# A three-part network on one core: norms split into two stages, both layers written out, and the shift out of PSUM shared by ScalarE and VectorE

## The chip, the cores and the metric

The kernel runs on one core of one Trainium2 chip. The metric is the device time of one execution in microseconds. TensorE is PE here, its weight loads are PEld, VectorE is DVE, ScalarE is ACT, GpSimd is POOL, and SyncE, which issues most transfers, is SP.

## What is computed

An input x of 256 tokens by 1024 features goes through two layers of one kind, then a middle part with two other mixers, then eight experts and a last norm. Everything is float32. Of the reference, cut to what matters here:

```python
for l in range(DEPTH):                                   # 2 layers
    mod = c_act @ w_ada[l] + b_ada[l]                    # 6 vectors of 1024
    sh1, sc1, gt1, sh2, sc2, gt2 = jnp.split(mod, 6, axis=-1)
    h = x * (1.0 + sc1) + sh1
    y = _token_mixer(h, w_in[l], b_in[l], ...)           # three kinds of attention
    x = _layernorm(ALPHA * x + gt1 * y, ln_g[l, 0], ln_b[l, 0])
    h = x * (1.0 + sc2) + sh2
    y = _conv_ffn(h, w_up[l], w_conv[l], b_conv[l], w_down[l])
    x = _layernorm(ALPHA * x + gt2 * y, ln_g[l, 1], ln_b[l, 1])
```

The middle part has the same frame without modulation: mixer, norm, FFN, norm, attention, norm, router.

## The kernel before

**Products.** Each float32 weight tile of 1 MB (128 x 2048) is split into a high and a low part: ACT copies it rounded to `W_high` (`high`, L1413), DVE subtracts that from the raw tile and writes `W_low` over it (`low`, L1780), both in two halves. Activations are split in the same way, and a product is three matmuls (L762 to L764). SP loads the tiles into a ring of four slots `W` in the order of the list `W_LOADS` (L631), and in between rows of biases, gains and so on into a ring of four slots `R` (L636); it stops at the first load whose slot is not free. `W_high` has two slots, and ACT waits until PE is done with the tile before the last. PSUM has eight banks, given out in a ring in the order in which PE's jobs stand.

**Modulation.** `w_ada` comes in twelve chunks of 512 columns. DVE multiplies and adds a chunk in eight steps (`ada`, L1825 and L1827); PE sums over the partitions (`ada_column` L877 for shifts and scales, which land as columns in `modc`; `ada_row` for gates). Chunks 0 to 3 are the first thing in a layer and come through the ring `W`. Chunks 4 to 9 stand between the first six chunks of the mixer's input product ("A" and "B"), 10 and 11 between the `down` tiles; these come through two slots of their own, which POOL loads (L732).

**One layer.** PE transposes x (`transposes`, L819), ACT applies scale and shift on the way out of PSUM, four activations a bank (L1434), and rounds the result to `hT_high` (L1438); DVE makes `hT_low` (L1800) bank by bank. A bank holds one token block of 128 (t = 0, 1) and four of the eight feature tiles (q = 0, 1). Then come the A and B chunks, attention with the C and gate chunks in the background, the projections, the `out` product, and DVE's `residual` and `layernorm("ln1")`. After it x is transposed again, and `up` (22 tiles) and `down` (11 tiles, 22 rows of four 512-wide banks) follow, with `hidden_conv` on DVE for each up tile. The layer ends with `residual` and `layernorm("ln2")`. The two layers are one loop on every engine; the middle part is straight code.

**The norm.** `residual` takes the four banks one by one (L1913, L1915, and the statistics L1872). `layernorm` joins the statistics (L1880, L1882), ACT takes the root (L1473), DVE inverts and normalises both token blocks whole (L1886), and multiplies by the gain and adds the bias, half by half (L1894, L1896). Only then does `h_ready` let PE transpose that half.

The `down` loop closes all four banks with its last row:

```python
                        for j, (_, t, n) in enumerate(jobs):
                            last = product(acc[j][:, :], ...
```

## Time and profile before

| | us |
|---|---|
| median of 3 runs (lowest, highest) | 3110.49 (3108.21, 3115.19) |
| the profiled execution | 3112.35 |
| its span on the core | 3110.7 |
| PE busy in the span | 2692.7 (87%) |
| DVE busy | 2210.7 (71%) |
| ACT busy | 1471.9 (47%) |
| mean granted clock of PE | 0.908 |

The profiled execution's time is 1.65 us over its span, which is launch and end. PE's and DVE's busy times are spread unevenly: from about 2090 us on, the experts keep PE at 99 to 100% and the transfers at 320 to 370 GB/s; before that PE has stretches without work between the stages.

### The profile page before, as it was taken

The page shows a single profiled execution, that of the slowest core. Times are in us where ns is not written, and L with a number is a line of the kernel's source. Part 1 is how long each engine was busy: PE and PEld are TensorE (multiplying, and loading weights), DVE is VectorE, ACT ScalarE, POOL GpSimd, SP SyncE. Part 2 cuts the span into 40 slices and gives each one's busy share as a digit, 9 for nine tenths or more (in the row PEclk, how much of TensorE's full clock was granted, in tenths as well). Part 3 has the DMA queues.
Part 4 walks back from the last instruction along what each step waited for, and adds up shares of the span by engine and source line. Part 5 has one row for each costly group of instructions (what it writes and reads, how often), then busy time and mean ns, then how long its engine had stood idle before and what let it go on. Part 6 is the DMA issues. An engine that isn't in the chain of part 4 may idle for free.

```text
span 3110.7 us, 39930 instructions
## 1 busy us (share of the span) xinstructions
PE 2692.7 (87%) x13946; PEld 2286.7 (74%) x13946; DVE 2210.7 (71%) x2764; ACT 1471.9 (47%) x1677; POOL 19.6 (1%) x38
## 2 busy tenths in 40 slices
PE   5888877976888769968888996759999999999997
PEld 4766757965666659958787975658888888888885
DVE  6666656868666657855576545459889898898986
ACT  3243434423244334425333423337777777777774
POOL 0000000000000000000000000000000000000000
PEclk7899988987899889978898987669999999999998
DMA  8633335558533335533204563129898898898985
GB/s 316 253 139 122 137 121 179 185 184 310 215 127 122 132 125 190 198 128 109 82 15 146 178 228 119 55 97 363 343 364 341 340 365 340 337 366 339 370 337 210
DMA packets 104027, 670.75 MB, mean 216 GB/s; under 512 B 11920, under 2 KB 12048, under 8 KB 26432
## 3 DMA queue, kind: packets, MB, share of 16 engines
q1 hardware_dynamic: 98032, 629.95, 54.8%
q0 software_dynamic: 5840, 38.80, 3.3%
q8 instruction: 90, 1.47, 0.2%
q14 instruction: 65, 0.53, 0.0%
HBM read 664.51 MB, written 4.19 MB: 215 GB/s over the span
## 4 chain that ended last, share of the span: by engine, by line
PE 52%; DVE 16%; PEld 16%; issue 8%; ACT 5%; DMA 2%; DVEq 0%; PEldq 0%; SPq 0%; ACTq 0%
PE bank L762 15%; PE bank L763 15%; PE bank L764 15%; PEld bank L764 5%; PEld bank L762 5%; PEld bank L763 5%; DVE W_low L1780 4%; PE bank L1064 3%; DVE work L1827 2%; ACT W_high L1413 1%; DMA W<-in_w_expert 1%; ACT scores L1459 1%; PEld bank L1295 1%; DVE scores L1967 1%; PE bank L819 1%
## 5 line engine op out<-in xcount | busy, mean ns | idle before, releaser
L1780 DVE TENSOR_TENSOR W_low<-W,W_high 128x1024 fp32r<-128x1024 f32 (+2 forms) x448 | 519.9, 1203 | 373.3 <-ACT W_high L1413 366.3
L1413 ACT ACTIVATE W_high<-W 128x1024 fp32r<-128x1024 f32 (+2 forms) x448 | 442.9, 1037 | 669.1 <-PE bank L764 272.0
L763 PE MATMUL bank<-W_low,arena_parts 128*128 128x512 f32 x1224 | 481.9, 394 | 0.0
L762 PE MATMUL bank<-W_high,arena_parts 128*128 128x512 f32 x904 | 365.0, 404 | 26.9 <-DVE work L2282 20.2
L762 PE MATMUL bank<-W_high,hT_high 128*128 128x512 f32 (+4 forms) x784 | 322.6, 412 | 47.0 <-DVE arena L1767 19.0
L764 PE MATMUL bank<-W_high,arena_parts 128*128 128x512 f32 x904 | 357.2, 395 | 0.0
L762 PE MATMUL bank<-hT_high,W_high 128*128 128x256 f32 x1184 | 344.3, 291 | 13.7 <-DVE hT_low L1800 11.8
L763 PE MATMUL bank<-hT_low,W_high 128*128 128x256 f32 x1184 | 340.2, 287 | 0.0
L764 PE MATMUL bank<-hT_high,W_low 128*128 128x256 f32 x1184 | 339.9, 287 | 0.0
L763 PE MATMUL bank<-W_low,hT_high 128*128 128x512 f32 (+4 forms) x784 | 311.5, 397 | 0.0
L764 PE MATMUL bank<-W_high,hT_low 128*128 128x512 f32 (+4 forms) x784 | 310.6, 396 | 0.0
L762 PE MATMUL bank<-arena_parts 128*128 128x512 f32 x672 | 272.5, 406 | 1.9 <-DVE arena_parts L2762 1.9
L763 PEld LDWEIGHTS bank<-W_low,arena_parts 128*128 128x128 f32 x1224 | 233.2, 191 | 48.5 <-issue 1.0
L764 PE MATMUL bank<-arena_parts 128*128 128x512 f32 x672 | 263.8, 392 | 0.0
L762 PEld LDWEIGHTS bank<-hT_high,W_high 128*128 128x128 f32 x1184 | 232.6, 196 | 14.9 <-issue 12.6
L763 PEld LDWEIGHTS bank<-hT_low,W_high 128*128 128x128 f32 x1184 | 233.3, 197 | 0.0
L764 PEld LDWEIGHTS bank<-hT_high,W_low 128*128 128x128 f32 x1184 | 232.5, 196 | 0.0
L763 PE MATMUL bank<-arena_parts 128*128 128x512 f32 x576 | 225.3, 391 | 0.0
L762 PEld LDWEIGHTS bank<-W_high,hT_high 128*128 128x128 f32 x784 | 162.7, 208 | 83.6 <-DVE arena L1767 20.3
L1445 ACT ACTIVATE arena_parts<-W 128x2048 fp32r<-128x2048 f32 x96 | 184.4, 1920 | 81.7 <-DMA W<-in_w_expert 63.0
L762 PEld LDWEIGHTS bank<-W_high,arena_parts 128*128 128x128 f32 x904 | 172.8, 191 | 65.0 <-issue 22.7
L1787 DVE TENSOR_TENSOR W_low<-W,arena_parts 128x2048 fp32r<-128x2048 f32 x96 | 217.9, 2283 | 3.0 <-ACT arena_parts L1445 3.0
(338 smaller groups left out, 4491.1 us busy)
## 6 DMA issues: line engine op xcount, KB each, us to landing
W<-in_w_expert SPq DMA_DIRECT2D x192, 1024.0 KB, 4.8
W<-in_w_layer SPq DMA_DIRECT2D x178, 1024.0 KB, 5.0
arena<-in_w_expert SPq DMA_DIRECT2D x144, 1024.0 KB, 4.8
W<-in_w_middle SPq DMA_DIRECT2D x58, 1024.0 KB, 5.0
arena<-in_w_layer POOLq DMA_DIRECT2D x32, 1024.0 KB, 7.6
R<-in_rows_layer SPq DMA_DIRECT2D x70, 256.0 KB, 5.8
R<-in_rows_middle SPq DMA_DIRECT2D x18, 256.0 KB, 6.1
spread<-arena POOLq DMA_DIRECT2D x1, 3072.0 KB, 11.9
```

Of the source, the lines that this page charges most:

```text
L762: mm(bank, lhs[0], rhs[0], start=start, stop=False)
L763: mm(bank, lhs[0], rhs[1], start=False, stop=False)
L764: return mm(bank, lhs[1], rhs[0], start=False, stop=stop)
L819: last = turn_over(bank[:, i * P:(i + 1) * P], src[:, t, f:f + P], ident)
L1064: last = mm(bank[:, i * P:(i + 1) * P], lhs(i), rhs(i), start=True, stop=True)
L1295: last = turn_over(bank[:, i * P:(i + 1) * P], hid_tok[:, c % 2, i * P:(i + 1) * P], ident)
L1413: do(high_slot(a.at, w)[:, cols], raw(a.at, w)[:, cols], ACT.Copy).then_inc(main_highs.filled[main_highs.slot(a.at, w)], 1)
L1445: do(expert_high(j), expert_raw(j), ACT.Copy).then_inc(stream.raised, 1)
L1459: i = do(scores[:, b, m, 0:K], scores[:, b, m, 0:K], ACT.Exp, bias=nmax[:, b, m:m + 1], accum_out=rsum[:, b, m:m + 1])
L1780: tt(lows(v.at, w)[:, cols], raw(v.at, w)[:, cols], high_slot(v.at, w)[:, cols].bitcast(F32), ALU.subtract).then_inc(*low_ready.event(v.at))
L1787: tt(expert_low(j), expert_raw(j), expert_high(j).bitcast(F32), ALU.subtract).then_inc(stream.lowered, 1)
L1827: i = stt(acc, part, csil[:, f:f + 1], acc, ALU.mult, ALU.add)
```

## The change

- **Both layers are written out** (`layer0`, `layer1`), each with its own lists of loads.
- **The modulation of the next layer moves into this layer's FFN.** Layer 0 computes, after chunks 10 and 11, also chunks 0 to 3 of layer 1 (called `next`), in steps of one DVE instruction placed between up tiles and between down tiles (`ada_steps`), and loads them over POOL's queue. Chunks 10 and 11 move from the down tiles to the up tiles.
- **The norm has two stages.** `norm` only subtracts the mean and divides, in four quarters, each with its own signal to PE. Gain and bias are folded into the modulation (`fold`), or are taken from columns in the middle part (`lnc`), and applied with it on the way out of PSUM. `scale_x`, which multiplies x itself by gain and adds bias, comes later: in the up tiles 0 and 1, or behind the transposes. `residual` joins the statistics of token block 0 before it takes the last bank.
- **Out of PSUM**: ACT scales and shifts token block 1 (`high_shifted`), DVE block 0 (`shifted`); ACT rounds both. This holds for all seven norms with a product behind them, also those of the middle part, where ACT had copied the bank to `hT_high` directly.
- **`down`** keeps its order for nine tiles; the last two tiles are done bank by bank, so that the banks close one after the other.
- **The first two weight tiles behind a norm** are split before the norm, with their high part in a free piece of the arena (`EARLY`, `high_next`, `low_next`).
- **SP** loads rows two tiles later than before, and loads the constants and x at the start behind the first two tiles of chunk 0. The lambda row is handled behind chunk A0. The convolution taps are copied aside. The output goes out in two halves.

The core of the diff:

```diff
+LAYERS = tuple(f"layer{l}" for l in range(DEPTH))
+PASSES = (("start", 1),) + tuple((p, 1) for p in LAYERS) + (
+    ("middle", 1), ("expert", NE - 1), ("last", 1), ("over", None), ("end", 1))
...
+    for j in range(FF1 // P):
+        loads += [("up", j, 0)]
+        if j in (9, 10):
+            loads += [("ada", j + 1, i) for i in range(2)]
+        if j > 10 and j % 2 == 0 and j < 18 + 2 and l + 1 < DEPTH:
+            loads += [("next", NEXT[(j - 12) // 2], i) for i in range(2)]
+    return loads + _halves("down", FF1 // 256, 1)
...
+        EARLY = {("layer0", ("up", 0, 0)): 10256, ("layer0", ("up", 1, 0)): 12304,
+                 ("layer1", ("up", 0, 0)): 10256, ("layer1", ("up", 1, 0)): 12304,
+                 ("layer1", ("A", 0, 0)): 2048, ("layer1", ("A", 0, 1)): 16400,
+                 ("middle", ("ba", 0, 0)): 2048, ("middle", ("qkv", QKV[0], 0)): 16400,
+                 ("middle", ("up", 0, 0)): 6144, ("middle", ("up", 1, 0)): 8192,
+                 ("middle", ("wq", 0, 0)): None}
...
+                    if name == ("ada", 0, 1):
+                        first()
+                    while due and due[0][1] <= 0:
+                        row(due.pop(0)[0])
+                    if name[:2] in R_LOADS[at.part] and name[:2] + (1 - name[2],) not in loads[n:]:
+                        due.append((name[:2], 2))
...
+            def first_inputs():
+                sp.dma_start(consts[:, :], ins["constants"]).then_inc(consts_in, 16)
+                sp.dma_start(x[:, :, :], ins["x"].rearrange("(t p) d -> p t d", p=P)).then_inc(x_in, 16)
...
+                for c in range(tiles // 2 - 2):
+                    for k in (2 * c, 2 * c + 1):
+                        ready(k)
+                        for j in range(4):
+                            last = row(k, j)
...
+                    last.then_inc(*weights.frees(at, ("down", c, 0)))
+                    between(c)
+                for j in range(4):
+                    for k in range(tiles - 4, tiles):
+                        if j == 0:
+                            ready(k)
+                        last = row(k, j)
+                        if j == 3 and k == tiles - 3:
+                            last.then_inc(*weights.frees(at, ("down", tiles // 2 - 2, 0)))
+                    last.then_inc(*psum.fills(at, jobs[j]))
...
+            def high_shifted(name, scale, shift):
+
+                for q in range(2):
+                    f = slice(4 * q, 4 * q + 4)
+                    act.wait_ge(*psum.full(a.at, (name, 1, q)))
+                    bank = banks[psum.slot(a.at, (name, 1, q))]
+                    for i in range(4):
+                        n = 4 * q + i
+                        o = do(hT[:, n, P:S], bank[:, i * P:(i + 1) * P], ACT.Identity,
+                               scale=modc[:, scale + n:scale + n + 1], bias=modc[:, shift + n:shift + n + 1])
+                    o.then_inc(*psum.frees(a.at, (name, 1, q)))
+                    for t in range(NT):
+                        act.wait_ge(*psum.vacated(a.at, (name, t, q)))
+                        cols = slice(t * P, (t + 1) * P)
+                        do(hT_high[:, f, cols], hT[:, f, cols], ACT.Copy).then_inc(*group_high.event(a.at))
...
+            def roots():
+
+                for t in range(NT):
+                    state["var"] += 1
+                    act.wait_ge(*var_ready.nth(a.at, state["var"]))
...
+            def shifted(name, scale, shift):
+
+                for q in range(2):
+                    dve.wait_ge(*psum.full(v.at, (name, 0, q)))
+                    bank = banks[psum.slot(v.at, (name, 0, q))]
+                    for i in range(4):
+                        f = 4 * q + i
+                        o = ts(hT[:, f, 0:P], bank[:, i * P:(i + 1) * P], scale[:, f:f + 1], shift[:, f:f + 1],
+                               ALU.mult, ALU.add)
+                    o.then_inc(*psum.frees(v.at, (name, 0, q)))
+                    for t in range(NT):
+                        state["group"] += 1
+                        dve.wait_ge(*group_high.nth(v.at, state["group"]))
+                        f, cols = slice(4 * q, 4 * q + 4), slice(t * P, (t + 1) * P)
+                        tt(hT_low[:, f, cols], hT[:, f, cols], hT_high[:, f, cols].bitcast(F32), ALU.subtract
+                           ).then_inc(*group_split.event(v.at))
...
+            def ada_steps(l):
+
+                chunks = [("ada", 10), ("ada", 11)] + [("next", c) for c in NEXT if l + 1 < DEPTH]
+                for m, (kind, c) in enumerate(chunks):
+                    acc = ada_acc[:, m % 2, :]
+                    if m > 1:
+                        dve.wait_ge(*psum.full(v.at, chunks[m - 2] if m < 4 else ("next", m - 4)))
+                    for f in range(KD):
...
+            def fold(g, b, sh, sc, to):
+
+                tt(modc[:, to:to + 8], modc[:, g:g + 8], modc[:, sc:sc + 8], ALU.mult).then_inc(dve_done, 1)
+                dve.wait_ge(dve_done, v.count())
+                tt(modc[:, to + 8:to + 16], modc[:, b:b + 8], modc[:, sc:sc + 8], ALU.mult).then_inc(dve_done, 1)
+                dve.wait_ge(dve_done, v.count())
+                tt(modc[:, to + 8:to + 16], modc[:, to + 8:to + 16], modc[:, sh:sh + 8], ALU.add).then_inc(dve_done, 1)
...
+            def norm(signal=None):
+
+                def invert(t):
+                    state["std"] += 1
+                    dve.wait_ge(*std_ready.nth(v.at, state["std"]))
+                    V.reciprocal(inv[:, t:t + 1], inv[:, t:t + 1]).then_inc(dve_done, 1)
                     dve.wait_ge(dve_done, v.count())
...
+                        if n == 0:
+                            invert(t)
+                        half = x[:, t, n * 512:(n + 1) * 512]
+                        i = ts(half, half, meanvar[:, t, 0:1], inv[:, t:t + 1], ALU.subtract, ALU.mult)
+                        if signal is None:
+                            i.then_inc(dve_done, 1)
+                            dve.wait_ge(dve_done, v.count())
+                        else:
+                            i.then_inc(*signal.event(v.at))
+                if signal is not None:
+                    dve.wait_ge(*signal.last(v.at))
...
+            def scale_x(at, name, n, signal=None):
+
+                dve.wait_ge(*rows.full(at, (name, f"g{n}")))
+                g = R[:, rows.slot(at, (name, f"g{n}")), :]
+                dve.wait_ge(*rows.full(at, (name, f"b{n}")))
+                b = R[:, rows.slot(at, (name, f"b{n}")), :]
+                half = x[:, :, n * 512:(n + 1) * 512]
+                tt(half, half, g.unsqueeze(1).to_broadcast([P, NT, 512]), ALU.mult).then_inc(*rows.frees(at, (name, f"g{n}")))
+                dve.wait_ge(*rows.vacated(at, (name, f"g{n}")))
+                tt(half, half, b.unsqueeze(1).to_broadcast([P, NT, 512]), ALU.add).then_inc(*rows.frees(at, (name, f"b{n}")))
+                dve.wait_ge(*rows.vacated(at, (name, f"b{n}")))
+                if signal is not None:
...
+                    if n:
+                        stat(t)
...
+                norm(h_ready)
+                shifted("h2T", modc[:, 64:72], modc[:, 72:80])
+                steps_ = ada_steps(l)
...
+                def between_up(j):
+                    if j < 2:
+                        scale_x(v.at, "ln1", j)
+                        return
+                    for _ in range(2 if j > 9 and j % 2 else 1):
+                        next(steps_, None)
+                    if j == 17:
+                        ada_in(10)
+                    if j == 20:
+                        ada_in(11)
+
...
+                hidden_conv(FF1 // P, hid1, taps_kept, between_up)
+                for c in range(FF1 // 256 - 2):
+                    low(1)
+                    for _ in range(3):
+                        next(steps_, None)
+                    if c == 0 and l + 1 < DEPTH:
+                        dve.wait_ge(*rows.full(v.at, ("nextc", 0)))
+                        V.tensor_copy(modc[:, 0:16], R[:, rows.slot(v.at, ("nextc", 0)), 0:16]
+                                      ).then_inc(*rows.frees(v.at, ("nextc", 0)))
+                        dve.wait_ge(*rows.vacated(v.at, ("nextc", 0)))
+                    if l + 1 < DEPTH and c in (1, 5, 8):
+                        next_in(c // 3)
+                if l + 1 < DEPTH:
+                    next_in(3)
+                    fold(48, 56, 0, 8, 80)
```

Three places in the order of the instructions. First DVE at the end of layer 0, before: the last bank of the `down` residual, the norm, and its gains and biases (L1889 and L1891 are waits for rows).

```order
L1913 TENSOR_TENSOR work<-bank,arena 128x512
L1915 SCALAR_TENSOR_TENSOR x<-x,work 128x512
L1872 BN_STATS small<-x 128x6
L1880 BN_AGGR small<-small 128x2 x2
L1882 TENSOR_SCALAR small<-small 128x2
L1868 RECIPROCAL small<-small 128x2
L1886 TENSOR_SCALAR x<-x,small 128x1024 x2
L1889 ISA
L1894 TENSOR_TENSOR x<-x,R 128x2x512
L1896 TENSOR_TENSOR x<-x,R 128x2x512
```

The same place in the changed kernel; L2025 is the statistics, L2047 the quarter of the norm, L1891 the shift out of PSUM, L1898 the low part, L2063 and L2065 `scale_x`.

```order
L2025 BN_STATS small<-x 128x6
L2030 BN_AGGR small<-small 128x2
L2032 TENSOR_SCALAR small<-small 128x1
L2039 RECIPROCAL small<-small 128x1
L2047 TENSOR_SCALAR x<-x,small 128x512
L2039 RECIPROCAL small<-small 128x1
L2047 TENSOR_SCALAR x<-x,small 128x512 x3
L2521 ISA
L1891 TENSOR_SCALAR hT<-bank,modc 128x128 x4
L1898 TENSOR_TENSOR hT_low<-hT,hT_high 128x4x128 x2
L1891 TENSOR_SCALAR hT<-bank,modc 128x128 x4
L1898 TENSOR_TENSOR hT_low<-hT,hT_high 128x4x128 x2
L2063 TENSOR_TENSOR x<-x,R 128x2x512
```

The gains and biases have moved behind the shifts, and the chunks 0 to 3 that followed in the loop are gone from here. Second, DVE in one up tile of layer 0, in the changed kernel (up tile 11; L1871 is the split of a weight tile, L2119 to L2123 the convolution, L2099 to L2103 the end of the tile before, L1964 a step of a `next` or `ada` chunk).

```order
L1871 TENSOR_TENSOR W_low<-W,W_high 128x1024 x2
L2119 TENSOR_SCALAR work<-bank,taps_kept 128x256
L2121 SCALAR_TENSOR_TENSOR work<-bank,taps_kept,work 128x255
L2123 SCALAR_TENSOR_TENSOR work<-bank,taps_kept,work 128x254
L2099 TENSOR_TENSOR acted<-acted,bank 128x256
L2101 CAST arena_parts<-acted 128x256
L2103 TENSOR_TENSOR arena_parts<-acted,arena_parts 128x256
L1964 SCALAR_TENSOR_TENSOR arena<-arena,small 128x512 x2
```

Before, the same tile ended with its seventh row (L1933 there). The up tiles 2 to 10 have one step, from 11 on every odd one has two. Third, DVE before the residual of `down` in layer 0, in the changed kernel:

```order
L1871 TENSOR_TENSOR W_low<-W,W_high 128x1024 x2
L1979 SCALAR_TENSOR_TENSOR modc<-bank,modc 128x4 x2
L1985 TENSOR_TENSOR modc<-modc 128x8
L1987 TENSOR_TENSOR modc<-modc 128x8
L1989 TENSOR_TENSOR modc<-modc 128x8
L1871 TENSOR_TENSOR W_low<-W,arena_parts 128x1024 x4
L2081 TENSOR_TENSOR work<-bank,arena 128x512
```

The split of the next layer's first two tiles (the row with x4) now stands ahead of the first residual bank.

## Rows read from the trace of the kernel before

**Rows 1.** Windows: busy time of each engine in five stretches; columns in the first line.

```profile
core 0: us, PE busy (x) PEld busy (x) DVE busy (x) ACT busy (x) POOL busy (x), PEclk, DMA share, GB/s
486.10:612.00 125.90, 125.89 (x1032) 125.90 (x1033) 98.52 (x159) 51.82 (x63) 1.06 (x2) 0.99 0.55 191
612.00:676.80 64.80, 64.80 (x295) 53.11 (x293) 45.30 (x57) 22.22 (x23) 1.06 (x2) 1.00 0.58 204
676.80:731.00 54.20, 11.16 (x50) 10.40 (x49) 42.72 (x62) 9.41 (x16) 1.06 (x2) 0.54 0.72 257
731.00:792.60 61.60, 51.07 (x221) 40.80 (x221) 50.42 (x65) 23.07 (x32) 4.11 (x8) 0.92 0.78 298
1359.40:1390.70 31.30, 3.72 (x17) 3.32 (x17) 19.05 (x29) 4.89 (x9) 0.00 (x0) 0.57 0.34 118
```

**Rows 2.** Timeline, PE, layer boundary: start us, busy us, what [idle before <-releaser].

```profile
696.74 3.67 PE L819 MATMUL bank<-consts,x 128*128 128x128 f32 x16 [19.91 <-DVEq L1991]
...
723.30 1.87 PE L877 MATMUL bank<-consts,work 128*128 128x1 f32 x8 [4.79 <-DVEq L1835]
731.00 0.79 PE L762 MATMUL bank<-W_high,hT_high 128*128 128x512 f32 x1 [5.84 <-DVE hT_low L1800]
```

**Rows 3.** Timeline, DVE, the four residuals before that boundary.

```profile
674.83 0.69 DVE L1913 TENSOR_TENSOR work<-bank,arena 128x512 f32<-128x512 f32 x1 [5.70 <-PE bank L764]
...
682.82 0.69 DVE L1872 BATCH_NORM_STATS2 small<-x 128x6 f32<-128x512 f32 x1
```

**Rows 4.** Timeline, PE, first layer, from the mixer to the FFN.

```profile
475.25 1.97 PE L819 MATMUL bank<-consts,x 128*128 128x128 f32 x8 [13.84 <-DVEq L1898]
...
486.11 0.58 PE L762 MATMUL bank<-hT_high,W_high 128*128 128x256 f32 x1 [5.92 <-DVE hT_low L1800]
```

**Rows 5.** Timeline, DVE, the same place.

```profile
468.61 0.69 DVE L1872 BATCH_NORM_STATS2 small<-x 128x6 f32<-128x512 f32 x1
...
470.89 1.66 DVE L1886 TENSOR_SCALAR x<-x,small 128x1024 f32<-128x1024 f32 x2
472.58 1.22 DVE L1894 TENSOR_TENSOR x<-x,R 128x1024 f32<-128x1024 f32 x1
```

**Rows 6.** Timeline, ACT, the same place.

```profile
476.40 1.50 ACT L1434 ACTIVATE hT<-bank,modc 128x128 f32<-128x128 f32 x4 [6.17 <-PE bank L819]
477.94 0.63 ACT L1438 ACTIVATE hT_high<-hT 128x512 fp32r<-128x512 f32 x1
```

**Rows 7.** Timeline, DVE, up tiles of the first layer, and one ada chunk.

```profile
610.74 2.36 DVE L1780 TENSOR_TENSOR W_low<-W,W_high 128x1024 fp32r<-128x1024 f32 x2 [0.71 <-ACT W_high L1413]
...
616.53 2.36 DVE L1780 TENSOR_TENSOR W_low<-W,W_high 128x1024 fp32r<-128x1024 f32 x2 [0.69 <-ACT W_high L1413]
618.81 0.54 DVE L1948 TENSOR_SCALAR work<-bank,R 128x256 f32<-128x256 f32 x1
...
630.06 2.33 DVE L1827 SCALAR_TENSOR_TENSOR work<-arena,small,work 128x512 f32<-128x512 f32 x3
```

**Rows 8.** Timeline, DVE, lambda row at the start of layer 1.

```profile
736.27 0.28 DVE L2014 TENSOR_TENSOR scores<-R 128x128 f32<-128x128 f32 x1
```

**Rows 9.** Timeline, PE, layer 1, before the second B chunk.

```profile
792.57 0.79 PE L762 MATMUL bank<-W_high,hT_high 128*128 128x512 f32 x1 [9.26 <-DVE arena L1767]
```

**Rows 10.** Timeline, PE, middle part, the norm behind its mixer.

```profile
1656.42 1.97 PE L819 MATMUL bank<-consts,x 128*128 128x128 f32 x8 [11.88 <-DVEq L1898]
...
1663.22 0.58 PE L762 MATMUL bank<-hT_high,W_high 128*128 128x256 f32 x1 [1.91 <-DVEq L1808]
```

**Rows 11.** Timeline, PE, middle part, the norm behind its FFN.

```profile
1886.45 1.97 PE L819 MATMUL bank<-consts,x 128*128 128x128 f32 x8 [14.78 <-DVEq L1898]
```

**Rows 12.** Timeline, DVE, start of the program.

```profile
13.78 0.49 DVE L1825 TENSOR_SCALAR work<-W,small 128x512 f32<-128x512 f32 x1 [13.66 <-DMA W<-in_w_layer]
```

**Rows 13.** Timeline, PE, first matmul on weights.

```profile
48.44 0.79 PE L762 MATMUL bank<-W_high,hT_high 128*128 128x512 f32 x1 [5.83 <-DVE hT_low L1800]
```

**Rows 14.** Timeline, SP queue, the output.

```profile
3106.22 0.41 SPq L715 DMA_DIRECT2D out_x<-x  x1
```

673 lines of the change are left out of this document (364 added, 309 removed).

## The prediction

> **What bounds the kernel now.** I read the windows first. In the FFN of layer 0 PE works without a break at full clock, while DVE is busy 98.5 of 125.9 us in the up tiles and 45.3 of 64.8 in the down tiles [rows 1]. Between the layers PE is busy 11.2 of 54.2 us, and before the middle part 3.7 of 31.3 [rows 1]. So there are two kinds of places: stages that PE bounds, where other engines have cover, and boundaries, where one chain over DVE, ACT and PE sets the time. The change shortens the boundaries and pays with DVE work in the covered stages; the question is whether the cover is large enough.
>
> The PE timeline gives the boundary of the layers: the last down matmul ends at 696.74 - 19.91 = 676.83, the first product of layer 1 starts at 731.00 [rows 2]. In between DVE takes four residual banks, norms, gains, the loop's turn and four chunks of modulation. The same view for the mixer-to-FFN boundary: `out` ends at 475.25 - 13.84 = 461.41, `up` starts at 486.11, 24.7 us [rows 4]. In the A and B chunks at the start of a layer PE is busy 51.1 of 61.6 us, and its one long wait, 9.26 us, ends with a DVE evacuation [rows 1, 9]: that stage is DVE's, and work put on DVE there shows in full.
>
> **The chain of the new norm.** I count from a = end of the last statistics. Join and epsilon 0.45; inverting 0.2 (ACT's root of block 0 is done, that of block 1 falls beside it); the quarters are 0.41 each, since two whole blocks took 1.66 [rows 5]. With another 0.2 for block 1 the first quarter is done at a+1.1, the second at a+1.75, the last at a+2.7. Four transposes take 0.98 (eight took 1.97 [rows 4]): block 1 of the first half is in PSUM at a+3.1. ACT shifts it in 1.50 and rounds two banks in 0.63 each [rows 6]: a+6.05. DVE's low part of block 0 stands behind the first, of block 1 behind the second: a+6.2 and a+6.9. The second half comes 3.3 us later (a+9.5, a+10.2), since ACT's 1.50 and DVE's four shifts follow in turn.
> The one price not in the trace is DVE's shift, 128x128 out of PSUM. The nearest row is the same operation on 256 columns, 0.54 [rows 7]; four of 0.16 (the smallest instructions) to 0.54 are 0.6 to 2.2 us. I take 0.30 each, 1.2 together, nearer the half-size operation. It is not on the path except at the start of the program: DVE is free at a+2.7 and done before ACT's 4.6.
> The Trainium skill ("VectorE: DVE Perf Modes", the section on the TRN2 errata) gives PSUM-to-SBUF costs by which four shifts are an estimated 1.03 us on VectorE and 1.00 on ScalarE. For ScalarE the trace has 1.50. With the page's values for both, each norm would come some 0.5 us sooner, about 4 us in all.
>
> **Part by part**, gains with a minus.
> 1. *Layer 0 to layer 1.* The last 12 rows x 4 of `down` change: two tiles, 10.9 us, are done bank by bank, so a bank closes every 2.7 us. DVE first has to split the next layer's two tiles; their second raw tile can only be loaded once down tile 8 is done, 10.9 us before the end; with some 4 us of landing and 3.4 of split DVE is free about 4 us before the end. Three residuals of 2.18 us (four took 682.82 + 0.69 - 674.83 = 8.7 [rows 3]) and the last bring a to end + 5.0. The first product waits for a+6.25: 11.2 us instead of 54.2. **-43.0**.
> 2. *Layer 1 to the middle part.* The same a; its first chunk needs all four banks, a+10.3: 15.3 instead of 31.3 [rows 1]. `scale_x` behind it (four of 1.22 [rows 5]) lies beside that chunk's product. **-16.0**.
> 3. *Mixer to FFN, twice.* a was 468.61 + 0.69 = 469.30, `up` came 16.8 later [rows 4, 5]; now 6.95: -9.85. Joining block 0 early costs 0.4. The residual's second pair started 3.5 us behind PE's end because a weight split that waited for PE stood before it (4.36 us of residual end at 469.30, so it began at 464.9); the early high parts free about 2.0 of it. -11.4 each, **-22.8**.
> 4. *Middle part.* Mixer to FFN: transposes to product were 6.8 us, with the same norm before them; `up` came 12.3 after a [rows 10], now 6.95, and the residual begins 3.4 sooner, minus 0.4: -8.4. Behind its FFN [rows 11] the residual still waits for a split that waits for PE, so only the norm gains: -2.9. Router: all four banks are needed, -1.6. **-12.9**.
> 5. *End.* The output is issued at 3106.22 [rows 14]; the first half leaves earlier, the second at the same time. Bounds 0 and 2. **-1**.
> 6. *Start.* DVE began at 13.78, when some 4 MB had landed [rows 12]. Now chunk 0 comes first, but DVE then needs the columns behind it, and ahead of those stand four weight tiles, constants and x, 7.4 MB. At the same rate they land at about 23.3; before, DVE went on at about 20.3, after eight steps of 0.8. +3 us. Then block 0's shift and the rounding stand behind DVE's weight split, where ACT had worked beside it, +2.1. **+5.1** on 48.44 [rows 13]; bounds -5 (DVE's first step comes some 7 us sooner, and the wait for the columns might not last) and +9 (everything lands later still).
> 7. *A and B chunks, twice.* The lambda row, about 1.5 us from its first instruction [rows 8], moves from a pause into DVE's busy stage, and the next weight's high part now queues on ACT behind it, another 0.8. **+4.6**.
> 8. *Up tiles.* A tile takes PE 5.75 us; DVE waits 0.69 of it for ACT's high part [rows 7], so it works 5.1. A step is 0.8 (three took 2.33 [rows 7]). A tile's low part may be 3.3 us late before PE notices: 5.75 less 1.2 for ACT's half and 1.2 for DVE's. The two `scale_x` add 5.0 in tiles 0 and 1: DVE is 2.5 behind, 3.5 after tile 9 (eight steps), and in layer 0 the last twelve tiles carry 18 steps, 14.4 us against 8 of slack: 9.7 behind. Less 3.3: +6.4. Entering the down tiles late costs 1.0. In layer 1 the steps end with tile 15: +2.5. **+9.9**. Bounds 0 and the whole added work, 44.
> 9. *Down tiles.* Four `next` columns on PE: 1.87 each at the low clock [rows 2], half at the high, +3. The bank-by-bank end needs all rows of the last tile at once, but its high part waits for tile 8: about 1.4 us of wait, three times, +4.2. **+7.2**.
>
> What else is hidden: 8 MB over POOL's queue fall into stages where the transfer engines are 55 to 58% busy [rows 1]; without that cover a tile is about 3 us at the start's rate [rows 12]. Rows two loads later still precede their use by more than a landing. SP stops at the first row of layer 1 until `scale_x`, but four weight tiles are ahead of it.
>
> Sum: -43.0 - 16.0 - 22.8 - 12.9 - 1 + 5.1 + 4.6 + 9.9 + 7.2 = -68.9. The profiled execution was 3112.35 us, giving 3043.4; it stood 1.9 over the median of 3110.49. I say **3042**.
>
> **The rivals.**
> - *DVE becomes the bound in the up tiles for all it is given* (chance 0.12): a late low part passes on through ACT's order, and the slack of 3.3 us isn't there. For it: three engines hand each tile on in turn. Against: DVE now waits in every tile. Then +44 instead of +9.9: 3076.
> - *The chains overlap better* (0.14): the start costs nothing, PE never waits for a late split in the up tiles or at the end of `down`. -5.1 - 9.9 - 4.2 in full: 3023; half of it: 3033.
> - *Slower: PE's clock falls in the up tiles* (0.04). In the up tiles it is held at 0.99 by unbroken work [rows 1]; if the waits for DVE let it fall to the 1.2 GHz level, matmuls there take double, as the first behind a pause does (0.58 [rows 4]). Two up stages are 252 us; the 69 us gained are lost from a mean clock of 0.785 down. At 0.75 the stages cost 84 more: 3126. Against: in the A and B chunks PE waits for DVE too, and the clock was 0.92 [rows 1]. The Trainium skill ("TensorE: Matmul & The Clock Gate", "HAM oscillation") warns of this pattern, repeated waits that throttle PE; by the 0.92 it doesn't bite here.
> - *The boundaries don't close* (0.03): the early high parts don't come in time, because their raw tiles wait for SP. Then the old order of split and norm costs some 15 us at each of the two large boundaries: 3072.
>
> **The numbers.** Forecast 0.67, with its own range 3030 to 3056 from the bounds of the start and the up tiles. 8 in 10 takes in half of the better overlap and most of the DVE-bound case: 3022 to 3070. A measurement of this kernel can tell 0.2%, 6.2 us, from no change. Only the clock case, or several bad cases together, ends near or above 3104: faster 0.94, same 0.02, slower 0.04.
>
> **What would show it.** Right: the PE gap between the layers is 10 to 13 us, that before the middle part 14 to 17, those before the two layers' `up` 13 to 14 instead of 24.7; DVE shows no idle time in the up tiles 10 to 21 of layer 0 and PE short waits for `W_low` there. Wrong: PE without waits there (then 3033), or DVE-bound from the first tile (3076); a PE gap between the layers over 20 us; a clock under 0.9 in an up stage; the first product before 48 us.

## The result: 3079.98 us, faster, but 38 us short of the forecast

| | before | after |
|---|---|---|
| median, us (lowest, highest) | 3109.68 (3108.21, 3115.19), 4 runs | 3079.98 (3078.56, 3081.78), 4 runs |
| ratio to before, 95% interval | | 0.9902 [0.9884, 0.9919] |
| profiled execution, its span | 3112.35, 3110.7 | 3081.78, 3080.0 |
| PE busy | 2692.7 | 2696.3 (88%) |
| DVE busy | 2210.7 | 2236.1 (73%) |
| ACT busy | 1471.9 | 1470.6 (48%) |
| mean granted clock of PE | 0.908 | 0.919 |

The change is faster by 1.0%. The forecast was 3042 with a range of 3022 to 3070, so the sign was right and the size was not: 30.7 us of span were gained where the sum had 68.9. A second comparison of the same two kernels on another chip, in the experiments below, gave 0.9893 [0.9878, 0.9908].

### The profile page after: what moved, and what is told of

It is laid out like the page before. It is cut to its first block, busy times and chain, and to the rows that moved or that the text cites. A ratio compares the mean times of both kernels' runs of the same rounds, so it can differ in the third digit from the quotient of the medians.

```text
span 3080.0 us, 38153 instructions
## 1 busy us (share of the span) xinstructions
PE 2696.3 (88%) x13946; PEld 2285.4 (74%) x13946; DVE 2236.1 (73%) x2873; ACT 1470.6 (48%) x1685; POOL 24.0 (1%) x46
## 4 chain that ended last, share of the span: by engine, by line
PE 43%; DVE 24%; PEld 17%; issue 8%; ACT 6%; DMA 2%; PEldq 0%; DVEq 0%; SPq 0%; ACTq 0%
PE bank L794 12%; PE bank L795 12%; PE bank L796 12%; DVE W_low L1871 8%; PEld bank L796 6%; PEld bank L794 5%; PEld bank L795 5%; PE bank L1136 3%; DVE work L1939 2%; ACT W_high L1482 2%; DMA W<-in_w_expert 1%; ACT scores L1542 1%; PE bank L851 1%; PEld bank L1366 1%; DVE arena L1964 1%
## 5 line engine op out<-in xcount | busy, mean ns | idle before, releaser
L1871 DVE TENSOR_TENSOR W_low<-W,W_high 128x1024 fp32r<-128x1024 f32 x426 | 496.0, 1207 | 328.3 <-ACT W_high L1482 321.6
L1482 ACT ACTIVATE W_high<-W 128x1024 fp32r<-128x1024 f32 x426 | 422.1, 1039 | 588.3 <-PE bank L796 284.3
L794 PE MATMUL bank<-W_high,hT_high 128*128 128x512 f32 (+3 forms) x744 | 304.2, 409 | 39.7 <-DVE arena L1861 20.9
L794 PE MATMUL bank<-hT_high,W_high 128*128 128x256 f32 x1072 | 312.3, 291 | 11.6 <-DVE arena L1861 8.8
L795 PE MATMUL bank<-hT_low,W_high 128*128 128x256 f32 x1072 | 307.3, 287 | 0.0
L796 PE MATMUL bank<-W_high,hT_low 128*128 128x512 f32 (+3 forms) x744 | 294.1, 395 | 0.0
L794 PEld LDWEIGHTS bank<-hT_high,W_high 128*128 128x128 f32 x1072 | 209.7, 196 | 16.4 <-issue 10.9
L795 PEld LDWEIGHTS bank<-hT_low,W_high 128*128 128x128 f32 x1072 | 210.0, 196 | 0.5 <-issue 0.5
L794 PEld LDWEIGHTS bank<-W_high,hT_high 128*128 128x128 f32 x744 | 152.3, 205 | 76.5 <-issue 42.2
```

The costliest lines, as they stand in the source:

```text
L794: mm(bank, lhs[0], rhs[0], start=start, stop=False)
L795: mm(bank, lhs[0], rhs[1], start=False, stop=False)
L796: return mm(bank, lhs[1], rhs[0], start=False, stop=stop)
L1482: do(high_slot(at, w)[:, cols], raw(at, w)[:, cols], ACT.Copy).then_inc(main_highs.filled[main_highs.slot(at, w)], 1)
L1871: tt(lows(at, w)[:, cols], raw(at, w)[:, cols], high_slot(at, w)[:, cols].bitcast(F32), ALU.subtract).then_inc(*low_ready.event(at))
```

## The profile after, beside the rows of before

The windows of the changed kernel. The first two stretches are the FFN of layer 0 (up tiles; one column of the next modulation and the down tiles), the third is the boundary to layer 1, then the A and B chunks of layer 1 up to its long wait, the up tiles and down tiles of layer 1, and the boundary to the middle part. They answer to [rows 1].

```profile
core 0: us, PE busy (x) PEld busy (x) DVE busy (x) ACT busy (x) POOL busy (x), PEclk, DMA share, GB/s
478.60:620.80 142.20, 133.39 (x1060) 130.34 (x1060) 125.09 (x196) 53.44 (x67) 3.74 (x7) 0.98 0.59 213
620.80:691.50 70.70, 67.67 (x296) 55.42 (x296) 48.12 (x67) 20.95 (x22) 3.74 (x7) 0.95 0.67 239
691.50:716.80 25.30, 3.71 (x17) 3.34 (x17) 17.95 (x32) 8.62 (x15) 0.00 (x0) 0.60 0.42 164
716.80:779.50 62.70, 49.64 (x221) 39.03 (x221) 56.45 (x75) 21.88 (x27) 4.23 (x8) 0.95 0.78 289
1141.30:1283.00 141.70, 135.88 (x1060) 132.75 (x1060) 121.06 (x190) 53.95 (x68) 2.11 (x4) 0.95 0.52 190
1283.00:1345.50 62.50, 60.71 (x264) 49.33 (x264) 28.72 (x32) 20.52 (x21) 0.00 (x0) 1.00 0.44 152
1345.50:1372.50 27.00, 3.67 (x17) 3.27 (x17) 19.08 (x39) 9.18 (x19) 0.00 (x0) 0.66 0.21 78
```

Two things stand out. The boundaries did shrink (54.2 to 25.3, 31.3 to 27.0), but neither is near its forecast of 11.2 and 15.3. And the up tiles, where PE had worked without a break, now take 142 us instead of 129: DVE is busy 125.1 of 142.2 us there, and PE now has stops.

Reading PE's first and last matmul of each stage in both traces gives the whole ledger (a stage's change in us, gains with a minus; the sum differs from the 30.7 of the spans by rounding):

| stage | forecast | measured |
|---|---|---|
| start, to the first product | +5.1 | +2.5 (48.44 to 50.99) |
| A and B chunks, two layers | +4.6 | +3.3 (2.2 and 1.1) |
| mixer to FFN, two layers | -22.8 | -24.2 (24.7 to 12.6, twice) |
| up tiles, two layers | +9.9 | **+25.7** (13.2 and 12.5) |
| down tiles and columns | +7.2 | +9.8 (9.0 and 0.8) |
| layer 0 to layer 1 | -43.0 | **-28.9** |
| layer 1 to the middle part | -16.0 | **-4.2** |
| middle part and end | -13.9 | -12.5 |
| the rest of the layers | 0 | -2.3 |
| sum | -68.9 | -30.8 |

Three lines hold the miss: the two boundaries lack 25.9 us, the up tiles cost 15.8 more. Everything else together is 3.5 better than forecast.

**The boundary.** PE's timeline, changed kernel: the last down matmul, then the first transposes, then the first product of layer 1 (compare [rows 2]).

```profile
691.09 0.39 PE L796 MATMUL bank<-W_high,arena_parts 128*128 128x512 f32 x1
711.86 3.68 PE L851 MATMUL bank<-consts,x 128*128 128x128 f32 x16 [20.39 <-DVE x L2047]
716.76 0.47 PE L794 MATMUL bank<-arena_parts,hT_high 128*128 128x512 f32 x1 [1.23 <-DVE hT_low L1898]
```

From the transposes on all goes as forecast. The 20.4 us ahead of them are DVE's; its timeline (the last row is the end of the statistics, the point a of the prediction):

```profile
682.99 0.17 DVE L1989 TENSOR_TENSOR modc<-modc 128x8 f32<-128x8 f32 x1
696.03 2.36 DVE L1871 TENSOR_TENSOR W_low<-W,arena_parts 128x1024 fp32r<-128x1024 f32 x2 [12.88 <-ACT arena_parts L1482]
699.47 2.36 DVE L1871 TENSOR_TENSOR W_low<-W,arena_parts 128x1024 fp32r<-128x1024 f32 x2 [1.07 <-ACT arena_parts L1482]
701.75 0.68 DVE L2081 TENSOR_TENSOR work<-bank,arena 128x512 f32<-128x512 f32 x1
...
710.03 0.69 DVE L2025 BATCH_NORM_STATS2 small<-x 128x6 f32<-128x512 f32 x1
```

"Lowering" a tile is making its low part. DVE stands idle for 12.88 us in front of the lowering of A(0,0), while the residual's banks close one after the other behind it (all four are full before it goes on), and its first residual starts 10.3 us after PE's end; a is end + 19.2, not end + 5.0. ACT and SP say why:

```profile
694.87 2.00 ACT L1482 ACTIVATE arena_parts<-W 128x1024 fp32r<-128x1024 f32 x2 [14.02 <-DMA W<-in_w_layer]
```

```profile
667.37 2.38 SPq L658 DMA_DIRECT2D R<-in_rows_layer  x4
690.15 2.73 SPq L653 DMA_DIRECT2D W<-in_w_layer  x4
```

ACT waits for the raw tile, and SP issues it only at 690.15, 1.3 us before the end of `down`. Its rows were long out (669.8), so what it waited for is a weight slot. The slot of a tile is its number *inside its part* modulo four. Layer 0 has 90 ring loads, 90 modulo 4 is 2, and layer 1 starts again at slot 0: A(0,0) takes the slot of down tile 9, A(0,1) that of down tile 10, and both are freed only by the last matmuls. Layer 1 has 82 loads, the same remainder, and the same is seen before the middle part (SP at 1344.13, DVE waiting 10.08 and 4.73 us).

**The up tiles.** PE's timeline: its two longest stops in and behind the up tiles of layer 0.

```profile
600.72 0.55 PE L794 MATMUL bank<-hT_high,W_high 128*128 128x256 f32 x1 [5.47 <-DVE arena L1861]
601.07 0.42 PE L795 MATMUL bank<-hT_low,W_high 128*128 128x256 f32 x1
...
623.52 1.81 PE L939 MATMUL bank<-consts,arena 128*128 128x1 f32 x8 [2.72 <-DVEq L1970]
625.19 0.77 PE L794 MATMUL bank<-W_high,arena_parts 128*128 128x512 f32 x1
625.76 0.63 PE L795 MATMUL bank<-W_low,arena_parts 128*128 128x512 f32 x1
```

The first waits for a *bank*: the product of the 11th ada chunk sat in one from up tile 12 on, and DVE reads it only behind tile 17 (L1861). The second waits for the sum of the first `next` chunk. DVE's timeline for one tile in the middle of the stage, back to back:

```profile
580.36 2.36 DVE L1871 TENSOR_TENSOR W_low<-W,W_high 128x1024 fp32r<-128x1024 f32 x2
582.64 0.54 DVE L2119 TENSOR_SCALAR work<-bank,taps_kept 128x256 f32<-128x256 f32 x1
...
585.49 0.75 DVE L1964 SCALAR_TENSOR_TENSOR arena<-arena,small 128x512 f32<-128x512 f32 x1
```

From 580.36 to the next lowering at 587.09 DVE has 5.1 us of work of its own, 0.78 for each step, and here 0.3 of waiting where one chunk ends and the next begins: a tile with one step is 5.9 us against PE's 5.75, one with two is 6.7. DVE falls behind in every tile, and PE runs into it where there is the least slack, which is not the low part.

## The experiments

All diffs are cut, and against the changed kernel where nothing else is said. The first four ran on one chip, with the kernel before at 3109.59 us.

**The ring of slots goes on over the parts** (`e1_ring`).

```diff
-        slot = i % self.n
+        slot = (i + self.shift.get(at.part, 0)) % self.n
...
+        weights.shift["layer1"] = len(RING_LOADS["layer0"]) % W_SLOTS
```

> One edit: the ring of four weight slots goes on from layer 0 into layer 1 and the middle part, instead of beginning again at slot 0. In the changed kernel tile A(0,0) takes the slot of down tile 9 and A(0,1) that of down tile 10, and both are loaded only when layer 0's last matmuls are done (SP issues them at 690.15; ScalarE waits 14.02 us for the first, VectorE's lowering ends at 696.03 + 12.88). Theory T1 (the slot is the cause of the two long boundaries): with the ring going on, the tiles are there, VectorE goes from the last down bank into its residual at once, the gap of TensorE between layer 0 and layer 1 falls from 25.3 to 11 to 12 us, that between layer 1 and the middle part from 27.0 to 15 to 16, and the kernel takes 3055 us (3051 to 3060). Rival R1a (the position of the lowering in VectorE's program is what counts, the tile comes late in any slot, since SP's rows and the transfer itself take longer): the gaps fall by less than 4 us each, 3072 or more. Rival R1b (the boundaries close, but the norm behind them then waits for the rows of gate and scale): gaps near 18 us, 3065.

Measured: 3059.66 us (3055.24 to 3060.88), ratio 0.9833 [0.9817, 0.985], 20 us under the changed kernel. Its windows at the two boundaries:

```profile
689.60:703.70 14.10, 3.71 (x18) 3.32 (x17) 12.39 (x27) 3.30 (x10) 0.00 (x0) 0.63 0.39 144
1333.30:1347.60 14.30, 3.40 (x16) 3.17 (x16) 12.15 (x29) 5.49 (x14) 0.00 (x0) 0.80 0.17 69
```

The gaps are 14.1 and 14.3 us instead of 25.3 and 27.0; the up and down tiles of both layers take the same within 0.2 us. T1 holds: one line of the slot's arithmetic is worth 24 us of gaps. Between the layers 3 us remain over the forecast of 11.2, and DVE's timeline shows where: it waits 2.68 us for the high part of the second tile.

```profile
686.39 2.36 DVE L1873 TENSOR_TENSOR W_low<-W,arena_parts 128x1024 fp32r<-128x1024 f32 x2 [2.68 <-ACT arena_parts L1484]
688.67 0.68 DVE L2083 TENSOR_TENSOR work<-bank,arena 128x512 f32<-128x512 f32 x1
```

**The banks freed sooner** (`e2_bank`).

```diff
-                    if j == 17:
+                    if j == 13:
                         ada_in(10)
-                    if j == 20:
+                    if j == 19:
                         ada_in(11)
```

> One edit: VectorE takes the products of the 11th ada chunk out of their bank behind up tile 13 instead of 17, and the 12th behind 19 instead of 20, in both layers. Theory T2 (the ada chunk that sits in a bank is what stops TensorE in the up stage): the wait of 5.47 us at 600.72 and that of 3.34 us at 1262.88 go, and with the first a part of the time at a lowered clock behind it; 8 to 12 us less, 3068 to 3072 us. Rival R2 (VectorE is the bound of the up stage, 116.6 of 133.4 us busy there, and TensorE only meets it at that place): the wait moves to other up tiles, as waits for a lowered tile, and the stage's length and the total stay within 3 us of 3080.

Measured: 3067.6 us (3065.68 to 3076.52), ratio 0.986 [0.9844, 0.9877]. The median is 0.4 under T2's range, but the profile bears T2 out only in layer 1, where the wait is gone and the up tiles take 136.6 us instead of 141.7. In layer 0 the up tiles take 138.0 instead of 142.3, and the column behind them waits 6.42 us instead of 2.72:

```profile
620.93 0.37 PE L939 MATMUL bank<-consts,arena 128*128 128x1 f32 x1 [6.42 <-DVEq L1970]
```

Up, column and down of layer 0 together are 212.5 against 212.9. There R2 is right in kind: the wait moved, though to the column and not to a low part. (The profiled run was the slowest of the four; the other three stand 8 to 11 us lower, and its stages can't tell why.)

**Layer 1 without steps in the up tiles** (`e3_layer1_steps`).

```diff
+                    if l:
+                        return
                     for _ in range(2 if j > 9 and j % 2 else 1):
                         next(steps_, None)
...
-                    for _ in range(3):
+                    for _ in range(2 if l else 3):
                         next(steps_, None)
```

> One edit: layer 1 goes back to two ada steps behind each down tile, none behind the up tiles, as the kernel before had them (its two last ada chunks are taken out behind down tile 5 and before the next part's tiles); layer 0 is left. It prices what the steps cost that VectorE does between up tiles. Theory T3 (VectorE is the bound of the up stage by these steps): up and down of layer 1 together fall from 204.2 us to 191 to 194, near the 190.8 of the kernel before, total 3068 to 3071. Rival R3 (the 16 steps cost the same wherever they stand, since VectorE's load over up and down together is unchanged): 201 us or more, total 3077 to 3081.

Measured: 3062.76 us (one run). Up and down of layer 1 take 131.1 and 62.8 us, 194.5 with the 0.5 between them, where T3 had 191 to 194. The windows of this kernel's layer 1:

```profile
1136.30:1267.40 131.10, 129.66 (x1056) 129.19 (x1056) 108.91 (x173) 53.88 (x68) 1.05 (x2) 0.97 0.53 189
1267.90:1330.70 62.80, 62.52 (x268) 49.88 (x268) 39.68 (x48) 20.25 (x21) 1.06 (x2) 1.00 0.51 185
```

T3's stages hold within 0.5 us: 16 steps cost 10.5 us among the up tiles (8.4 against a second profile of the changed kernel, below) and 0.9 among the down tiles. The run's total, 5 us under T3's range, is 17 under the changed kernel; 9.7 are this edit, and some 5 lie in the mixer of layer 0, where the code is the same. One run can't tell that from scatter.

**The residual ahead of the lowering** (`e4_residual_first`).

```diff
+                residual(DOWN, 2, ALPHA)
                 low_next(LAYERS[l + 1] if l + 1 < DEPTH else "middle", 2)
-                residual(DOWN, 2, ALPHA)
```

> One edit: at the end of both layers VectorE does the residual of the FFN before it lowers the first two tiles of the next part; the ring of slots stays as it is. It tells the order in VectorE's program apart from the late tile itself. Theory T4 (TensorE waits because the residual stands behind a lowering that waits for a late tile; the tile is there by the time the norm is done): the gap between layer 0 and layer 1 falls from 25.3 to 15 to 17 us, that between layer 1 and the middle from 27.0 to 17 to 19, total 3060 to 3064. Rival R4 (the late tile alone sets the end: its landing and its lowering end so late that the order is of no use): gaps of 22 us or more, total 3074 or more.

Measured: 3063.54 us (one run), the gaps 16.0 and 17.9 us:

```profile
690.20:706.20 16.00, 3.42 (x17) 3.16 (x17) 11.60 (x21) 8.47 (x15) 0.00 (x0) 0.68 0.63 254
1332.20:1350.10 17.90, 3.67 (x16) 3.27 (x16) 12.64 (x28) 9.06 (x19) 0.00 (x0) 0.60 0.31 119
```

T4 holds at both places. The tile is as late as before, but DVE no longer stands in front of it with its residuals undone. So the cause of the long boundary has two halves, the late slot and the order in DVE's program; taking away either gives back 9 to 13 us a place.

The next four ran on a second chip, with the kernel before at 3112.93 us.

**ScalarE does both blocks** (`e5_all_act`). Shown is what DVE loses; ACT's loop over block 1 becomes one over both blocks.

```diff
                 for q in range(2):
-                    dve.wait_ge(*psum.full(v.at, (name, 0, q)))
-                    bank = banks[psum.slot(v.at, (name, 0, q))]
-                    for i in range(4):
-                        f = 4 * q + i
-                        o = ts(hT[:, f, 0:P], ...)
-                    o.then_inc(*psum.frees(v.at, (name, 0, q)))
                     for t in range(NT):
```

> One edit: ScalarE scales and shifts both token blocks out of PSUM, as in the kernel before; VectorE does none. Everything else of the change stays. It prices the split between the two engines. Theory T5 (the split is worth its share of the chain only): the first product comes 1.4 to 2.5 us earlier than 50.99, since VectorE's four shifts no longer stand in front of its low parts there while ScalarE waits; where a block's quarters come one after another the second shift of 1.50 us adds 1.5 to 3 us per norm on five norms inside the program. Total 3080 to 3090, around +5. Rival R5 (the split is most of what the rebuilt norms gain): each of the boundaries lengthens by 4 us or more, total 3100 or more. Rival R5b (the split costs, as VectorE is the busy engine): total under 3078.

Measured: 3090.12 us (3086.41 to 3090.55), ratio 0.9928 [0.9912, 0.9945]. The first product comes at 48.67 instead of 50.99, the gaps before the two `up` are 13.5 and 13.4 instead of 12.6, that before the middle part 28.7 instead of 27.0, the one between the layers is the same. Behind the middle part's mixer and at the router it is 0.8 and 1.0 longer, behind the middle part's FFN 0.6 shorter. T5 has the start right and the direction; it had 1.5 to 3 us on each of five norms, and they cost 0.8 to 1.7. With the start, all this is about +2 us. Most of the rest of the total lies in the middle part's up and down tiles, 216 us at a granted clock of 0.93 here against 209.5 to 210.2 at 0.95 with the split. Whether the split causes that clock was not settled. What is shown, by one profile: the split is worth 0.8 to 1.7 us at five of the seven norms inside the program, nothing or less at the other two, and costs 2.3 at its start, and it is not what the rebuilt norms gain.

**The start** (`e6_start`).

```diff
                     if name == ("ada", 0, 1):
+                        row(("adac", 0))
+                        row(("lam", 0))
+                    if name == ("ada", 1, 1):
                         first()
```

> One edit: in layer 0 SP issues the columns of the ada bias and the lambda row right behind the first two weight tiles, and the constants and x two tiles later than now. Theory T6 (VectorE's idle 9.10 us up to 21.68 is the wait for those columns, which stand behind some 7 MB): VectorE goes on from about 13, and the first product comes at 45 to 48 instead of 50.99, total 3074 to 3077. Rival R6 (the weight tiles behind it set the pace at the start, so an earlier column only moves the wait to the next tile): the first product at 50 or later, total unchanged.

Measured: 3076.26 us (one run), first product at 50.95: R6. (The total lies in T6's range too, 4 us under the changed kernel, but not by the start.) DVE's timeline shows the wait move:

```profile
12.55 0.20 DVE L2173 COPY modc<-R 128x64 f32<-128x64 f32 x1 [0.24 <-DVE work L1943]
13.50 0.49 DVE L1941 TENSOR_SCALAR work<-W,small 128x512 f32<-128x512 f32 x1 [0.76 <-DMA W<-in_w_layer]
14.02 5.58 DVE L1943 SCALAR_TENSOR_TENSOR work<-W,small,work 128x512 f32<-128x512 f32 x7
28.23 0.16 DVE L2008 SCALAR_TENSOR_TENSOR modc<-bank,modc 128x4 f32<-128x4 f32 x1 [8.63 <-PE bank L926]
```

The columns are there at 12.55 instead of 21.68, but then the first ada column is late on PE, whose program has the transposes of x (now at 23.05) ahead of it.

**Layer 0's steps spread** (`e8_spread`).

```diff
-                    for _ in range(2 if j > 9 and j % 2 else 1):
+                    for _ in range(2 if l and j > 9 and j % 2 else 1):
...
-                    for _ in range(3):
+                    for _ in range(3 + (c + 1) % 2):
...
-                    if l + 1 < DEPTH and c in (3, 6, 8):
-                        next_column((c + 1) // 3)
+                    if l + 1 < DEPTH and c in (1, 4, 6, 8):
+                        next_column((1, 4, 6, 8).index(c))
```

> Layer 0 gives VectorE one ada step behind every up tile from 2 on (20 in all, instead of 26) and three or four behind every down tile; the first column of the next layer's modulation is taken by TensorE behind down tile 1 instead of up tile 21, the others behind 4, 6 and 8; the bank of the 11th ada chunk is freed behind up tile 13, the 12th's behind 19. Layer 1 keeps its steps and has the bank edit too. Theory T8 (in layer 0 VectorE is the bound of the up tiles: 5.1 us of own work a tile and 0.8 a step against TensorE's 5.75, and what waits at the bank or at the column is only where TensorE meets it): six steps fewer and no column at the end of the up tiles take 8 to 10 us off up and down of layer 0 (212.9 to 203 to 205), 5 off layer 1 as in the bank run, total 3063 to 3068. Rival R8 (the sum over up and down is what counts, steps moved to the down tiles come back there): layer 0 stays at 211 or more, total 3074 or more.

Measured: 3083.36 us (3082.13 to 3085.3), ratio 0.9907 [0.9891, 0.9924], no gain. T8 falls: the up tiles of layer 0 take 140.1 us, 2.1 *more* than in the bank run with six steps fewer, and the down tiles 77.4 instead of 66.3; up, column and down together 218.0 instead of 212.9. PE's timeline shows three stops:

```profile
596.24 2.08 PE L931 MATMUL bank<-arena,consts 128*128 128x512 f32 x2 [4.71 <-DVEq L1967]
...
632.69 1.86 PE L939 MATMUL bank<-consts,arena 128*128 128x1 f32 x8 [3.93 <-DVEq L1967]
...
679.76 1.61 PE L939 MATMUL bank<-consts,arena 128*128 128x1 f32 x8 [2.59 <-DVEq L1967]
```

Each waits for the *sum* of an ada chunk, which the slower rate of steps finishes too late for the fixed place of its product in PE's program. R8 is right that it comes back in the down tiles, for this reason.

**A price: one step in eight** (`e9_fewsteps`). Left out are seven of the eight additions of each of the six chunks (two in layer 1), so the modulation differs and the experts' part of the run can't be compared.

```diff
                         if f == 0:
-                            i = ts(acc, part, csil[:, 0:1], None, ALU.mult)
-                        else:
-                            i = stt(acc, part, csil[:, f:f + 1], acc, ALU.mult, ALU.add)
...
+                            ts(acc, part, csil[:, 0:1], None, ALU.mult).then_inc(dve_done, 1)
```

> A price, not a candidate: of the eight steps by which VectorE sums each ada chunk in the up and down tiles, only the first is done (seven of eight are left out, in the 11th and 12th ada chunk of both layers and in the four chunks for the next layer); loads, waits, rows and columns stay. Theory T9 (the added 32 us over the two FFNs are VectorE's steps and what follows from them): up and down of layer 0 take 194 to 198 us instead of 212.9 (the kernel before 190.7, plus four columns of TensorE), of layer 1 191 to 193 instead of 204.2, total 3048 to 3054. Rival R9 (a good part is something else, the two norm scalings in the first tiles, the early high parts, or transfers of the ada chunks over POOL's queue): 203 or more in layer 0, 197 or more in layer 1.

Measured: the total, 3201.04 us, says nothing, since PE does 14520 matmuls here instead of 13946, presumably by another routing. The stages do: up 132.2 and 131.8 us, down 65.5 and 61.9, with the column 199.9 in layer 0 and 194.2 in layer 1.

```profile
476.30:608.50 132.20, 129.28 (x1060) 127.63 (x1060) 111.02 (x177) 53.90 (x68) 3.74 (x7) 1.00 0.63 229
610.70:676.20 65.50, 65.17 (x288) 53.10 (x288) 29.38 (x40) 18.61 (x20) 3.17 (x6) 0.97 0.68 255
```

Between T9 (194 to 198, 191 to 193) and R9 (203, 197), nearer T9. The steps left out and what follows from them cost 10 us in each layer's up tiles (in layer 1 7.7 against the second profile of the changed kernel). About 3 us of the up tiles are not the steps: in layer 0 PE waits 1.69 for the second half of the norm in its first tile and 1.24 for the bank. And the down tiles of layer 0 keep 3.6 us over before though DVE is idle half the time there: those are the three columns on PE, not the bank-by-bank end, since layer 1, which has that end and no columns, takes 61.9, as before.

The last group of four ran on a third chip, with the kernel before at 3108.16 us.

**The changed kernel again** (`after_again`).

> The changed kernel itself, on the same chip as the next three runs, so that they can be read against it. Every theory expects 3078 to 3084 us and the same stages as in its first profile: 142 us of up tiles in layer 0, a gap of 25 us between the layers and of 27 before the middle part. In layer 1 the same up tiles took 141.65, 141.80, 139.43, 138.68 and 137.09 us in five profiles of kernels that have the same code there, with a granted clock of 0.85 to 1.00 in the stretch behind the bank wait; if that clock is what differs, this profile falls between 137 and 142 with the clock to match.

Measured: 3076.54 us (3075.58 to 3078.17), ratio 0.9893 [0.9878, 0.9908]. Every stage of layer 0 is within 0.2 us of the first profile. Layer 1's up tiles take 139.5 us, in the span expected, though the stretch behind the bank wait has the same clock as in the first profile, so that stretch alone does not explain the difference: in the first profile the first tiles stand at a mean clock of 0.91 (up to 1180), here at 1.00.

**Ring and residual in halves** (`e10_ring_halves`), beside the ring's edit:

```diff
-                low_next(LAYERS[l + 1] if l + 1 < DEPTH else "middle", 2)
-                residual(DOWN, 2, ALPHA)
+                coming_part = LAYERS[l + 1] if l + 1 < DEPTH else "middle"
+                low_next(coming_part, 1)
+                residual(DOWN[0:2], 2, ALPHA)
+                low_next(coming_part, 2, 1)
+                residual(DOWN[2:4], 2, ALPHA)
```

> The ring of slots goes on over the parts, as in the ring run, and besides VectorE lowers the first coming tile, does the residual of the first two banks, lowers the second tile, and does the other two banks. The ring run left 14.06 us between the layers where I had predicted 11.2: VectorE stood 2.68 us for ScalarE's high part of the second tile before its first residual. Theory T10 (that late second tile is the remaining 3 us): the gap between the layers is 10.5 to 12 us, that before the middle part at most 14.3, total 3050 to 3057. Rival R10 (VectorE's own work behind the last matmul, four residual banks and the norm, fills the 14 us): both gaps stay within 1 us of 14.1 and 14.3, total 3056 to 3060.

Measured: 3053.32 us (3051.9 to 3055.99), ratio 0.9818 [0.9803, 0.9833]; the gaps 11.3 and 13.4. T10 holds: with the tile in time and DVE not standing in front of it, the boundary is 11.3 us, the forecast's 11.2. DVE's timeline, PE's end being at 688.86:

```profile
687.53 2.35 DVE L1873 TENSOR_TENSOR W_low<-W,arena_parts 128x1024 fp32r<-128x1024 f32 x2
689.80 0.68 DVE L2083 TENSOR_TENSOR work<-bank,arena 128x512 f32<-128x512 f32 x1
...
693.42 0.69 DVE L2027 BATCH_NORM_STATS2 small<-x 128x6 f32<-128x512 f32 x1
```

The statistics end at 694.1, end + 5.25 (forecast: + 5.0).

**Bank and column out of the way** (`e11_column`), beside the bank edit:

```diff
-                    if j == 21 and l + 1 < DEPTH:
-                        hand_back()
-                        next_column(0)
...
-                    if l + 1 < DEPTH and c in (3, 6, 8):
+                    if l + 1 < DEPTH and c in (0, 3, 6, 8):
                         next_column((c + 1) // 3)
```

> The two edits on banks as in the bank run, and the first column of the next layer's modulation is taken by TensorE behind down tile 0 instead of up tile 21 (VectorE reads it behind down tile 2); the steps stay where the change has them, 26 in the up tiles and 22 in the down tiles of layer 0. Theory T11 (TensorE reached VectorE's backlog first at the bank, and with the bank freed sooner at the column; with neither in the way the backlog does not stop it, because the second half of a tile's low part comes later still): up 138 us, no wait at the column, down 67 to 69, up and down of layer 0 together 205 to 208 instead of 212.9, total 3062 to 3069. Rival R11 (VectorE is the bound, so the wait goes on to a low part or to a down tile): up and down of layer 0 at 211 or more, total as in the bank run or above it.

Measured: 3063.43 us (3060.43 to 3066.66), ratio 0.9854 [0.9838, 0.9869]. Up 137.9, then 1.8 of waiting for a low part, down 66.7: 206.4 together, 6.5 less than the changed kernel, as T11 says. The column waits for nothing now, and PE meets DVE's backlog only in low parts, in four waits of 1.6, 0.7, 0.5 and 1.8 us.

**Combined** (`c2_combined`): ring, halves, bank, column, layer 1's steps, layer 0's lambda row ahead of the chunks, and at the start columns and constants ahead of the lambda row and x.

> A candidate that should beat both kernels: ring going on over the parts with the residual in halves; banks and column as in the run before; layer 1's ada steps back behind the down tiles; layer 0's lambda row back in its old place ahead of the chunks; and at the start the ada columns, the constants and the lambda row right behind the first two weight tiles, x two tiles later (with the columns alone moved, VectorE went on at once but then waited 8.63 us for a product of TensorE, which needs the constants). By the stages measured so far: boundaries -28, layer 0's FFN -6, layer 1's -10, start -4 to -7, lambda row -1 to -2. If the gains add up: 3027 to 3036 us. If they share a resource (VectorE's backlog only moves): 3040 or more.

Measured: 3035.15 us (3034.39 to 3037.1), ratio 0.976 [0.9747, 0.9774]. The total is at the upper end of the 3027 to 3036 expected. The gains add up, with two exceptions: the first product still comes at 51.28, and the gap before the middle part is 17.3 instead of 13.4. SP's timeline shows the second: it stands in the four ln2 rows from 1288.19 to 1303.2, because the slot of the 12th ada row is read late, and the middle part's first tile is behind them.

```profile
1288.19 14.98 SPq L660 DMA_DIRECT2D R<-in_rows_layer  x4
1303.22 7.13 SPq L655 DMA_DIRECT2D W<-in_w_middle  x3
```

On a fourth chip, with the kernel before at 3112.68 us:

**Only the columns sooner** (`e12_start3`).

```diff
                     if name == ("ada", 0, 1):
+                        row(("adac", 0))
                         first()
+                        row(("lam", 0))
```

> The changed kernel with one edit at the start: only the ada columns are issued sooner, right behind the first two weight tiles, ahead of constants and x; the lambda row comes behind x. In the two runs before, x came two tiles later too, and TensorE did its transposes (start 23.05 and 23.38, behind x) ahead of the ada column, so that VectorE waited 8.63 and 4.11 us for that product. Theory T12 (of the start it is these two orders that cost: VectorE waits for the columns, and TensorE's program has the transposes of x ahead of the first ada column): VectorE goes on at 12.6 and waits only for the weight tile behind, first product at 46 to 48 instead of 50.9. Rival R12 (the weight tiles of the start land no sooner than VectorE needs them now): 50 or later.

Measured: 3074.97 us (one run), first product at 50.26, R12. DVE has the columns at 12.55 and then waits for the third weight tile:

```profile
21.18 0.49 DVE L1940 TENSOR_SCALAR work<-W,small 128x512 f32<-128x512 f32 x1 [8.43 <-DMA W<-in_w_layer]
```

Behind x and the constants that tile is there at 21.2, ahead of them at 13.5 (`e6_start`), and then x is late for PE. DVE and PE need both, and whichever is loaded second holds the chain: DVE has the first column's product at 28.2 us in `e6_start`, at 27.5 here. Letting PE take the ada column ahead of x's transposes would part the two; it was not tried.

**Combined, second form** (`c3_combined`): this start, and in layer 1, against the combined kernel,

```diff
+                    if l and c in (3, 6):
+                        ada_row(9 + c // 3)
...
-                    for _ in range(2 if l else 3):
+                    for _ in range(3):
                         next(steps_, None)
+                    if l and c in (4, 7):
+                        ada_in(9 + c // 3)
```

> The combined kernel with two edits more: the start as in the run beside it, and layer 1 does three ada steps behind each down tile instead of two, with TensorE's rows behind down tiles 3 and 6 and VectorE's additions behind 4 and 7. In the combined run SP stood 14.98 us in its four ln2 rows, up to 1303.2, because the row of the 12th ada chunk was read last; the middle part's first tile was late for it (VectorE waited 4.54 us for ScalarE), and the gap before the middle part was 17.3 us instead of 13.4. Theory T13 (rows read sooner let SP issue the tile in time): that gap is back at 13 to 14, the start gives 3 to 4, total 3026 to 3031 against 3035. Rival R13 (VectorE's three steps a tile hold back low parts in layer 1's down tiles, as with layer 0 in the run with spread steps): down of layer 1 at 65 or more instead of 62.9, total 3032 or more.

Measured: 3032.43 us (3031.53 to 3033.8), ratio 0.9742 [0.9729, 0.9755]: 2.6% under the kernel before, 1.5% under the changed one by their ratios. Its windows for the up and down tiles of layer 0 and the two boundaries:

```profile
473.10:611.00 137.90, 133.39 (x1060) 130.25 (x1060) 122.44 (x192) 53.47 (x67) 3.74 (x7) 0.98 0.62 220
612.80:679.40 66.60, 66.32 (x296) 53.90 (x296) 57.22 (x81) 26.39 (x28) 3.75 (x7) 0.97 0.76 283
679.40:690.70 11.30, 3.69 (x17) 3.28 (x17) 9.80 (x21) 3.07 (x9) 0.00 (x0) 0.70 0.45 180
1310.40:1324.00 13.60, 3.72 (x17) 3.28 (x16) 11.40 (x27) 5.29 (x13) 0.00 (x0) 0.63 0.18 73
```

The gap before the middle part is back at 13.6, so T13's first half holds. Layer 1's up and down take 128.9 and 63.8 us, 2 over before. The start gave 1.6 us against the combined kernel (first product at 49.65 instead of 51.28), not 3 to 4, and the total is 1.4 us over the upper end of T13. R13 has the total right (3032 or more) but not its reason: layer 1's down tiles take 63.8 us, not 65 or more.

## Why the prediction was wrong, step by step

1. *Layer 0 to layer 1, -43.0; measured -28.9.* The failed step is one clause: "their second raw tile can only be loaded once down tile 8 is done, 10.9 us before the end". It takes for granted that the ring of four goes on into the next layer. It starts anew, and with 90 loads the two coming tiles fall on the slots of down tiles 9 and 10. The number 90 modulo 4 could be had from `W_LOADS`. A second step fails with it: I let DVE be "free about 4 us before the end", and did not price what its residuals lose if the lowering ahead of them waits. The rest of that part is right: with tile and order mended the gap is 11.3.
2. *Layer 1 to the middle part, -16.0; measured -4.2.* The same clause, by 82 modulo 4. Mended it is 13.4, 1.9 better than my 15.3.
3. *Mixer to FFN, -22.8; measured -24.2.* Right, chain and size. The DVE shift of four measures 1.36 to 1.44 us, above both the 1.2 assumed and the 1.03 estimated beside it; it stands off the path here, as said.
4. *Middle part, -12.9, and 5, end, -1; measured together -12.5.* Right in sum, in part by two errors. The three norms gained 8.9, 3.7 and 2.3 where I had 8.4, 2.9 and 1.6, and the end 1.1; but the mixer and the FFN of the middle part took 1.8 and 1.6 us longer, for which I had no term. In the second profile of the changed kernel the mixer is 1.6 shorter than before and the FFN 1.2 longer, so at least the first is scatter.
6. *Start, +5.1; measured +2.5.* The direction is right. The shift on DVE cost its 2.1 (2.3 by the run in which ScalarE does both). The +3 for the columns was 0.2 to 0.6: they were read at 21.68, not at the estimated 23.3, and the kernel before, which read its own at 20.23, then waited for a weight tile, so that the last column's product is taken at 43.35 against 42.72.
7. *A and B chunks, +4.6; measured +3.3.* Near: 2.2 in layer 0 and 1.1 in layer 1, where I had 2.3 each. In `c2_combined` and `c3_combined`, where layer 0 has the lambda row and ACT's order as before, that stretch of layer 0 takes 61.3 and 61.2 us (61.6 before, 63.8 changed): in layer 0 the term is what I said it was. Why layer 1 pays half is open.
8. *Up tiles, +9.9; measured +25.7.* The backlog was priced well; where PE meets it was not. Two numbers fell. "A tile's low part may be 3.3 us late before PE notices" speaks of low parts alone; the bank of the 11th ada chunk and the column have no such slack, and cost 5.47 in layer 0, 3.34 in layer 1, and 2.72 at the column. And the clock was lower behind the first wait: 0.84 in the 20.8 us from there, some 3 us. With bank and column out of the way the up tiles of layer 0 cost +8.9 where I had +6.4, and those of layer 1 +5.4 where I had +2.5 (+7.4 in the two other runs with that edit); DVE is the bound in each tile by 0.15 us, and PE's first tile waits 1.7 us for the second half of the norm, which I had not counted.
9. *Down tiles, +7.2; measured +9.8.* Near in sum, by two errors. The bank-by-bank end costs nothing to speak of (layer 1: 61.93 us against 61.84). The columns cost more than 3: the first is 4.4 us with its wait, and the matmuls behind it take 0.63 us instead of 0.39 up to about 630.

**The rivals.** "The boundaries don't close", at 0.03, is what happened at both large boundaries, and its 15 us each were the right size (14.1 and 11.7 missing); its cause, raw tiles that wait for SP, is right, but it was the slot SP waited for. Its chance was too low, since it hung on one clause that I had not looked up. "DVE becomes the bound in the up tiles" is true in kind, at over half of the price: +25.7 of up tiles against +44, and a third, +14.3, once bank and column are out of the way. The clock case did not come, but its mechanism did in small.

The Trainium skill ("TensorE: Matmul & The Clock Gate", "HAM oscillation") warns that repeated waits throttle PE; I wrote that it does not bite here. The trace shows a lower clock behind a single wait, by 0.41 us instead of 0.28 for a matmul of 256 columns after the 5.47 us, and not as a lasting state: the whole up stage has 0.98.

## What to carry to other kernels

Where a change rests on a prefetch, look up the slot that the prefetched tile lands in: a ring whose index starts anew at a part's boundary makes the first tiles of the next part wait for the last of this one, however far ahead the code asks for them. Put a wait that may be long behind work that is ready: with the residual ahead of it, DVE's lowering was as late as before, and 9.3 of the 14.0 us came back. And when work is added to an engine that has a little slack per tile, look for every place where another engine needs a result of it at a fixed point (a bank, a sum, a row's slot), because the backlog shows there first, and moving the work elsewhere only helps if these points move with it.

## What the runs showed of the hardware that I had not expected

The same wait does not always bring the slower clock. In layer 1 PE stands 3.34 us for the same bank in two kernels with the same code there. First the changed kernel (matmul, then the window behind it), then the one with the residual first:

```profile
1262.88 0.55 PE L794 MATMUL bank<-hT_high,W_high 128*128 128x256 f32 x1 [3.34 <-DVE arena L1861]
1260.00:1283.00 23.00, 20.09 (x144) 19.91 (x144) 16.60 (x28) 7.70 (x10) 0.00 (x0) 0.85 0.40 138
```

```profile
1252.17 0.36 PE L794 MATMUL bank<-hT_high,W_high 128*128 128x256 f32 x1 [3.34 <-DVE arena L1861]
1251.00:1270.00 19.00, 17.55 (x144) 17.37 (x144) 15.28 (x25) 7.29 (x10) 0.00 (x0) 1.00 0.48 167
```

In the first, part of the stretch behind runs at 1.2 GHz and the mean is 0.85; in the second it stays at 2.4 GHz. Such differences make the same up tiles take 137.1 us in one profile and 141.7 in another, so a stage of this kernel can be told apart to some 4 us in one profile. Its gaps repeat better: over the profiles of kernels that don't change them, 12.6 to 12.7 us ahead of `up`, 27.0 to 27.2 before the middle part, and 25.1 to 26.2 between the layers.
